# Three narrow weight blocks of a three-layer network multiplied the other way round: weights stationary, tokens moving

## The reference

```python
# first kind, twice
h = rms_norm(x, norm_g)
u = h @ w_in        # (256, 2048) @ (2048, 15944); split into
# a_q a_k a_v a_z (512 each) | a_qi 512 | a_ki 64 | a_wi 8 | b_* | c_* | m_* | gates
...
rel   = relu(einsum('bqhd,bsd->bqhs', qi, ki) * 64 ** -0.5)
score = einsum('bqh,bqhs->bqs', wi * 8 ** -0.5, rel)       # then top 64 of it, sparse attention
# second kind, once
proj = rms_norm_2(x, g_mix) @ w_in                          # c_q 512 | c_kv 512 | k_r 64 | q_d k_d v_d 1024 each | gates
k_rope = apply_rope(rms_norm_2(k_r, g_k_rope), cos, sin)    # shared by the 8 heads of one attention
```

## Time and profile before

| | |
|---|---|
| median of 3 runs | 3395.77 us (3395.47 to 3395.79) |
| profiled execution, its own time | 3395.34 us |
| its span | 3393.5 us, 39757 instructions, mean granted clock 0.992 |
| PE | 3368.6 us busy (99%), 15526 matmuls |
| PEld | 2789.7 us (82%) |
| DVE | 1904.9 us (56%) |
| ACT | 1517.2 us (45%) |
| POOL | 278.4 us (8%) |
| DMA | 617.99 MB, 60.4% of the 16 engines' span on the main queue |

### The profile page before, as it was taken

How to read it: one execution, slowest core, us unless ns; L and a number is a source line. 1 busy time by engine, 2 the same in 40 slices (tenths; PEclk the granted TensorE clock), 3 DMA queues, 4 the chain that set the end, 5 groups by cost and what they waited for, 6 DMA issues and landing times.

```text
span 3393.5 us, 39757 instructions
## 1 busy us (share of the span) xinstructions
PE 3368.6 (99%) x15526; PEld 2789.7 (82%) x15526; DVE 1904.9 (56%) x2078; ACT 1517.2 (45%) x1923; POOL 278.4 (8%) x235
## 2 busy tenths in 40 slices
PE   8999999999999999999999999999999999999999
PEld 7878888888888788888888888887788888888887
DVE  5365655555554656555555555565555555555555
ACT  5345445444444454454444444454444444444443
POOL 0010231000000102220000001151000000000000
PEclk9899999999998999999999999999999999999999
DMA  7555555566665555555766665454465666666665
GB/s 263 162 169 162 167 173 168 175 213 194 188 198 174 167 163 169 171 165 171 216 194 192 192 211 169 143 177 141 148 213 186 191 187 192 192 188 191 192 192 168
DMA packets 321306, 617.99 MB, mean 182 GB/s; under 512 B 25056, under 2 KB 25440, under 8 KB 319968
## 3 DMA queue, kind: packets, MB, share of 16 engines
q1 hardware_dynamic: 321120, 615.45, 60.4%
HBM read 608.03 MB, written 7.34 MB: 181 GB/s over the span
## 4 chain that ended last, share of the span: by engine, by line
PE 98%; ACT 1%; DVE 1%; issue 0%; DMA 0%; SPq 0%; ACTq 0%; DVEq 0%
PE G L836 91%; PE PT L627 3%; PE PO L717 1%; PE PS L700 1%; ACT w_hi L850 1%; PE PS L678 0%; PE PS L744 0%; PE PS L743 0%; PE PS L702 0%; DVE w_lo L1068 0%; DMA arena<-in_mem 0%; PE PS L766 0%; ACT core L973 0%; DVE sig L1108 0%; DVE stat L1176 0%
## 5 line engine op out<-in xcount | busy, mean ns | idle before, releaser
L1068 DVE TENSOR_TENSOR w_lo<-raw,w_hi 128x1024 fp32r<-128x1024 f32 (+2 forms) x1150 | 1411.0, 1228 | 1440.5 <-ACT w_hi L850 1423.4
L850 ACT ACTIVATE w_hi<-raw 128x1024 fp32r<-128x1024 f32 (+2 forms) x1150 | 1200.0, 1045 | 1744.1 <-PE G L836 1736.7
L836 PE MATMUL G<-w_hi,xh 128*128 128x512 f32 (+1 forms) x3296 | 1306.4, 396 | 0.0
L836 PE MATMUL G<-w_hi,xl 128*128 128x512 f32 (+1 forms) x3296 | 1282.4, 389 | 0.0
L836 PE MATMUL G<-w_lo,xh 128*128 128x512 f32 (+1 forms) x3296 | 1280.3, 388 | 0.0
L836 PEld LDWEIGHTS G<-w_hi,xl 128*128 128x128 f32 x3296 | 626.5, 190 | 129.1
L836 PEld LDWEIGHTS G<-w_hi,xh 128*128 128x128 f32 x3296 | 626.9, 190 | 125.9 <-issue 7.3
L836 PEld LDWEIGHTS G<-w_lo,xh 128*128 128x128 f32 x3296 | 627.6, 190 | 119.6
L836 PE MATMUL G<-w_hi,yh 128*128 128x512 f32 x1304 | 516.6, 396 | 3.0 <-DVE w_lo L1068 3.0
L836 PE MATMUL G<-w_hi,yl 128*128 128x512 f32 x1304 | 509.6, 391 | 0.0
L836 PE MATMUL G<-w_lo,yh 128*128 128x512 f32 x1304 | 509.1, 390 | 0.0
(11 more groups left out here) (124 smaller groups left out, 1340.4 us busy)
## 6 DMA issues: line engine op xcount, KB each, us to landing
raw<-in_w_in SPq DMA_DIRECT2D x624, 512.0 KB, 3.7
raw<-in_w_gate_up SPq DMA_DIRECT2D x176, 512.0 KB, 3.7
raw<-in_w_down SPq DMA_DIRECT2D x88, 512.0 KB, 3.5
raw<-in_w_branch SPq DMA_DIRECT2D x64, 512.0 KB, 3.8
raw<-in_w_out SPq DMA_DIRECT2D x64, 512.0 KB, 3.9
raw<-in_w_mem_kv SPq DMA_DIRECT2D x32, 512.0 KB, 5.0
raw<-in_w_o SPq DMA_DIRECT2D x32, 512.0 KB, 3.6
raw<-in_w_o_dil SPq DMA_DIRECT2D x16, 512.0 KB, 3.6
```

What stands on the lines that cost most here:

```text
L836: mm = M.matmul(G[b % 2][:, t, 0:blk.width], a[:, blk.kk + k, tok], w[:, c % RING, j, 0:blk.width], start=(k == 0 and q == 0), stop=(k == ...
L850: A(w_hi[:, c % RING, :, 0:blk.width], raw[:, c % RING, :, 0:blk.width], ACT.Copy).then_inc(hi_done, 1)
L1068: V.tensor_tensor(w_lo[:, c % RING, :, 0:w], raw[:, c % RING, :, 0:w], w_hi[:, c % RING, :, 0:w].bitcast(F32), ALU.subtract).then_inc(lo_d ...
```

## The change

For the three narrow blocks (new kind "turned") a chunk is six matmuls instead of twelve: the weights, 72 or 64 columns, are stationary, and all 256 tokens are the moving operand. The sums then stand with the output columns on the partitions. ACT copies them to SBUF (`turned_out`, a stretch of `tmp`) and counts `gm_free`. A new stage `back`, two chunks after the block's end, turns them with two transposes into a `PT` tile, and ACT copies the two halves, scaled per token, to where the block's result stood before. `ki` moves from r+18 to r+19. TensorE (in `ki`) and POOL (for `wis` and for `kr`) wait for the `PT` tile of `back` to be read, instead of for the block's `gm_free`. Nothing of the loads, of the splits or of the other blocks changes. In the diff the first `back` and the loop with "turned" are TensorE's, the read-out and the second `back` are ACT's.

```diff
-        ins = [("a_qi", A0 + 2048, NB, "copy"), ("a_kw", A0 + 2560, IDX_DIM + IDX_HEADS, "copy")]
+        ins = [("a_qi", A0 + 2048, NB, "copy"), ("a_kw", A0 + 2560, IDX_DIM + IDX_HEADS, "turned")]
...
-        out.append(Block((n, 2), ("in2",), col, "x", 0, KD, "copy", width))
+        out.append(Block((n, 2), ("in2",), col, "x", 0, KD, "turned" if width < NB else "copy", width))
...
-        at(r + 18, "ki", l)
+        at(r + 17, "back", "a_kw", l)
+        at(r + 19, "ki", l)
...
+    at(r + 73, "back", "kr", 2)
     at(r + 93, "kr")
...
+        turned_out = tmp[:, 4096:4352]
...
+        def brought(eng, *name):
+            i = PT_OF["back", *name]
+            eng.wait_ge(pt_free[i % 2], i // 2 + 1)
...
+            def back(i, name, l):          
+                b = BLOCK[name, l]
+                w = BLOCKS[b].width
+                freed(pe, b)
+                if i >= 2:
+                    pe.wait_ge(pt_free[i % 2], i // 2)
+                for t in range(TT):
+                    mm = M.transpose(PT[i % 2][:, t * w:(t + 1) * w], turned_out[0:w, t * P:(t + 1) * P], ident[0:w, 0:w])
+                mm.then_inc(pt_full, 1)
+
             def ki(i, l):
-                freed(pe, BLOCK["a_kw", l])
+                brought(pe, "a_kw", l)
...
+                        if blk.kind == "turned":
+                            for q, (a, w) in enumerate(((ah, w_hi), (ah, w_lo), (al, w_hi))):
+                                mm = M.matmul(G[b % 2][0:blk.width, 0, 0:T], w[:, c % RING, j, 0:blk.width], a[:, blk.kk + k, :],
+                                              start=(k == 0 and q == 0), stop=(k == blk.kt - 1 and q == 2))
+                            continue
...
+                elif blk.kind == "turned":
+                    act.wait_ge(mm_done, blk.end)
+                    A(turned_out[0:blk.width, :], G[b % 2][0:blk.width, 0, 0:T], ACT.Copy).then_inc(gm_free[b % 2], 1)
...
+            def back(i, name, l):
+                b = BLOCK[name, l]
+                w, by, dst = BLOCKS[b].width, scale_of(b), dst_of(b)
+                copied(i, [(dst[:, t, :], P, t * w, (t + 1) * w, by[:, t:t + 1]) for t in range(TT)])
...
-                freed(pool, BLOCK["a_kw", l])
+                brought(pool, "a_kw", l)
...
-            freed(pool, BLOCK["kr", 2])
+            brought(pool, "kr", 2)
```

More of the change, by code:

```diff
@@ L234 @@
 FEEDS = ("mem_feed", "x_feed", "m_feed", "l_feed", "h_feed")
-PT_OF = numbered(lambda s: 2 if s[0] == "ki" or s[:2] == ("s_turn", "l") else int(s[0] in FEEDS + ("qi", "s_turn", "s_pt", "tail", "c_f", "c_q", "b_turn", "kr")))
+PT_OF = numbered(lambda s: 2 if s[0] == "ki" or s[:2] == ("s_turn", "l") else int(s[0] in FEEDS + ("qi", "s_turn", "s_pt", "tail", "c_f", "c_q", "b_turn", "kr", "back")))
 HI_OF = numbered(lambda s: int(s[0] in FEEDS + ("tail",)))
@@ L788, in between @@
                         tail(stage, PT_OF[stage])
+                    elif what == "back":
+                        back(PT_OF[stage], *args)
                     elif what == "ki":
```

## The result

The changed kernel takes 3367.05 us (median of 4, 3366.68 to 3368.23) against 3395.78: ratio 0.9918, 95% interval 0.9905 to 0.9931. That is 28.7 us less; 26.9 were forecast. The profiled execution took 3367.36 us, its span is 3365.6.

What follows compares the result with a forecast made beforehand. TensorE, 98% of the span, was taken to bound the kernel. Layers 25.8 plus kr 1.1 gave 26.9 us off the profiled 3395.34; with 0.43 added for the median, 3368.9 us, range 3361 to 3378.

Steps and rivals of the forecast that it cites:

- The step of the new matmul: All three narrow blocks: 0.115 us per 256-column matmul, its weight load hidden; 48 matmuls, 5.5 us per block.
- Loading and streaming in series: Rival, chance 0.03: the load is not hidden behind 256 columns, 0.30 us a step; 3387.6 us in all.
- several passes: Rival, chance 0.03: a 256-column matmul runs in several passes like plain fp32, 0.56 us each; slower, 3425 us.
- The layers: Narrow a_kw blocks of layers 0 and 1: each gains 13.1 us less 0.2, together 25.8 us, mostly from the clock.
- way back: Two transposes two chunks behind each narrow block, turning its result back: costs 0.2 us each time.
- a_q at 8.56 instead of 8.4: Layer 0: first wide chunk after the narrow block starts at 138.9 at the earliest, against 149.60 before.
- a wait of 1.5 instead of 1.8: Layers, ahead of a_q: TensorE newly waits 1.8 us for the wide chunk's load and split.
- second chunk: Layer 0, a_q's second wide chunk: starts at 142.05 instead of 155.16, a gain of 13.1 us.
- the first rival: Layers' blocks, chance 0.17: the clock still falls, costing 3.4 us per layer; 3375.7 us in all.
- The kr block: Third narrow block, held by a dilated head's softmax: gains 1.5 us, not 5.2; 1.1 net, bounds -1 and +6.
- Scores, transposes and weighted sum: Softmax steps inside kr's block: forecast 2.9, 7.6 and 11.9 us after its start, with two waits on ACT and DVE.
- the supply at 8.4: Layers: the ring's load and split of the next wide chunk, not TensorE, set a_q's start, 138.9 at the earliest.

Runs made afterwards that it cites:

- old_transposes: The kernel before, with four idle transposes of the identity added behind each chunk of the layers' narrow blocks: 3386.80 us, 11.6 less; ratio 0.9969.
- layers_again: Repeat run: the kernel before with only the layers' two blocks changed, kr left as it was: 3372.84 us, against 3367.23 for the changed kernel beside it.
- heads_four: The changed kernel with dilated heads 4 to 7 begun six chunks later and four chunks apart instead of five: 3366.26 us, against 3367.23 beside it.
- late_readout: The changed kernel with ACT reading a_qi out one chunk later: 3367.12 us, against 3366.84 for the changed kernel beside it.

## Why the prediction was right

**The step of the new matmul**: 0.115 forecast, 0.117 measured (18 in 2.10 us). The load is hidden: it is shorter with fewer stationary columns. Weight loads of the changed kernel by form (count, busy us, mean ns):

```profile
...
L861 PEld LDWEIGHTS G<-w_hi,xh 128*128 128x128 f32 x3200 | 601.2, 188 | 128.0 <-issue 10.5
...
L855 PEld LDWEIGHTS G<-xh,w_hi 128*72 128x72 f32 x32 | 4.5, 141 | 0.1
...
L855 PEld LDWEIGHTS G<-xh,w_hi 128*64 128x64 f32 x16 | 2.2, 135 | 0.1
...
```

Loading and streaming in series (0.30) and several passes (0.56) are both out.

**The layers**: 25.8 forecast after the way back, 25.6 by the landmarks. Each term held: a_q at 8.56 instead of 8.4, a wait of 1.5 instead of 1.8 (TensorE arrives 0.5 later, half of it because the second matmul behind each group of transposes comes 0.08 late), second chunk after 11.75 instead of 11.5, way back 0.1 instead of 0.2. ki and rel wait for nothing; POOL's wait for a_kw, 18.6 us, is hidden. The clock stayed at 1.00 through a wait of 1.5 us with the block's matmuls before it, so the first rival fell; old_transposes shows that transposes added to the old block kept its clock up, so those inside the new one give that rival no support. But the reason that I gave for it was weaker than it looked: kr's old block, with the same transposes and score matmuls in it, lost its clock in layers_again.

**The kr block**: 1.1 forecast, 1.2 by landmarks: 1.6 up to the weighted sum, 0.4 lost behind it. Scores, transposes and weighted sum came 2.75, 7.41 and 11.80 us after the start, forecast 2.9, 7.6 and 11.9. That the softmax on ACT and DVE holds it, and that under it lies the supply at 8.4, heads_four shows by taking the first away.

**What the sum missed** is the 1.5 us between layer 1 and kr: a half-clock stretch of 3.4 us in the profile of before that did not come after. I had allowed for such stretches in the spread and not in the sum. The profile of before has four such single stretches ahead of its last microseconds, that of after three. That no more than one went is luck and no work of the forecast: the one behind kr, which I counted in both, is in all three profiles of the changed kernel but not in that of late_readout. layers_again adds that kr's old block can itself fall into one of 10 us: the forecast's 1.1 us is what kr gives where the old block had kept its clock, as in the profile that I read, and 3.5 where it had lost it.

## What to carry to other kernels

A product with few columns costs its weight loads, so put the few columns on the stationary side and the long dimension on the moving one: half the matmuls here, at nearly the same step (0.117 us instead of 0.112). But look at the granted clock first: most of the gain was that TensorE, "busy" with narrow matmuls, had dropped to half speed, and then the wide work behind them ran at half speed too; streaming unused columns alone brought two thirds of it or more. And where short chunks get shorter, price them against the ring that feeds them and the stages placed among them, not against the engine's own time: 5.2 us of saved matmuls were worth 1.2 in the kr block.

## What the runs showed of the hardware

- At 72 columns per load the clock fell within 3.7 us of the block's start though TensorE was never idle; at 128 and at 256 columns it stayed at 1.00. Adding work (idle transposes) to the 72-column block also kept it at 1.00 and made the kernel 11.6 us faster.
- A float32r matmul with 64, 72 or 128 moving columns and 128 stationary ones steps 0.112 us at full clock, one with 256 moving ones 0.120; with 256 moving ones and 72 stationary it is 0.117, and 0.114 with 64.
- The same instructions of kr's old block ran at clock 1.00 in one kernel and at a mean of 0.80 in another, in which they began 25 us earlier. Single half-clock stretches of 3.4 us come and go from one kernel to the next in places that the edit does not touch, at some 1.5 us each.
- A wait of TensorE of 2.3 us was followed by clock 0.50 in the kernel before (2325.60) and stayed at 1.00 in heads_four (2174.40).
- A 512 KB load issued 0.7 us earlier, with three more behind it, let ACT start 0.1 us earlier in one layer and 0.8 in the other. Behind one another, ACT's splits of such loads started 1.33 us apart, each waiting for its transfer (2171.94, 2173.27 and 2174.61 in heads_four).
